# One plain pair instead of two at the start of the feed-forward, and three weight-sum jobs that begin when the sliding stage's caches are loaded

## The reference

```
h = x @ w_in                                  # q/k/v of both attentions, two gates
A = differential attention (8 heads), B = sliding-window attention (16 heads, 2 kv heads)
x = LayerNorm(ALPHA * x + (sigmoid(g_a) * (A @ w_branch_a) + sigmoid(g_b) * (B @ w_branch_b)) @ w_o)
x = LayerNorm(ALPHA * x + relu(x @ w_up) ** 2 @ w_down)       # w_up 1024 x 4096, w_down 4096 x 1024
```

## Time and profile before

| | |
|---|---|
| median of three runs | 2153.51 us (2150.11 to 2153.92) |
| the profiled execution | 2153.98 us, its span 2152.2 us |
| TensorE (PE) busy | 2122.7 us, 99% of the span |
| VectorE (DVE) busy | 1470.2 us, 68% |
| ScalarE (ACT) busy | 1229.0 us, 57% |
| GpSimd (POOL) busy | 65.2 us, 3% |
| DMA | 399.27 MB, mean 186 GB/s |
| mean granted TensorE clock | 0.994 of full speed |

### The profile page before, as it was taken

The page is one execution under the profiler, slowest core; times in us unless marked ns, Lnnn a source line. Parts: engine busy times, 40 slices in busy tenths (PEclk is TensorE's granted clock), DMA queues, the critical chain, the costliest instruction groups (busy, mean ns, idle before and its releaser), DMA issues.

```text
span 2152.2 us, 38215 instructions
## 1 busy us (share of the span) xinstructions
PE 2122.7 (99%) x15004; PEld 1940.8 (90%) x15004; DVE 1470.2 (68%) x2336; ACT 1229.0 (57%) x2493; POOL 65.2 (3%) x100
## 2 busy tenths in 40 slices
PE   9999999999999999999999999998899999999998
PEld 7998889999989898989889888898899898989897
DVE  6757778667879356665767677785668793566646
ACT  4457776587535356656234677674875353556561
POOL 1000000000000000000010000000000000000000
PEclk9999999999999999999999999999999999999999
DMA  8876567984351855454268775479842517554541
GB/s 262 246 271 251 209 240 208 269 261 109 94 186 45 237 155 173 146 170 138 103 215 235 286 253 200 182 230 258 242 119 84 186 57 230 158 171 153 171 148 69
DMA packets 100866, 399.27 MB, mean 186 GB/s; under 512 B 15272, under 2 KB 16936, under 8 KB 87600
## 3 DMA queue, kind: packets, MB, share of 16 engines
q1 hardware_dynamic: 67904, 191.55, 26.0%
q0 software_dynamic: 7936, 92.28, 17.2%
q10 hardware_dynamic: 24848, 112.99, 14.7%
HBM read 367.42 MB, written 118.23 MB: 226 GB/s over the span
## 4 chain that ended last, share of the span: by engine, by line
PE 93%; DMA 2%; ACT 2%; issue 1%; DVE 1%; ACTq 0%; DVEq 0%
PE PS L828 9%; PE PS L830 8%; PE PS L829 8%; PE PS L1049 7%; PE PS L1050 7%; PE PS L1051 7%; PE PS L917 5%; PE PS L918 5%; PE PS L919 5%; PE PS L987 3%; PE PS L988 3%; PE PS L989 3%; PE PS L861 3%; PE PS L863 3%; PE PS L862 3%; PE PS L1177 2%
## 5 line engine op out<-in xcount | busy, mean ns | idle before, releaser
L828 PE MATMUL PS<-xt_hi,w_hi 128*128 128x320 f32 x1184 | 384.2, 325 | 8.8 <-ACT rope_s L1628 8.6
L830 PE MATMUL PS<-xt_hi,w_lo 128*128 128x320 f32 x1184 | 367.6, 310 | 0.0
L829 PE MATMUL PS<-xt_lo,w_hi 128*128 128x320 f32 x1184 | 367.5, 310 | 0.0
L2541 DVE TENSOR_TENSOR w_lo<-w_raw,w_hi 128x1024 fp32r<-128x1024 f32 x146 | 176.7, 1221 | 149.0 <-ACT w_hi L1579 147.6
L2548 DVE TENSOR_TENSOR w_lo<-w_raw,w_hi 128x1024 fp32r<-128x1024 f32 (+1 forms) x176 | 199.2, 1138 | 114.9 <-ACT w_hi L1595 114.6
L1579 ACT ACTIVATE w_hi<-w_raw 128x1024 fp32r<-128x1024 f32 x146 | 152.8, 1059 | 175.5 <-PE PS L1051 155.6
L828 PEld LDWEIGHTS PS<-xt_hi,w_hi 128*128 128x128 f32 x1184 | 224.6, 190 | 14.3 <-ACT rope_s L1628 9.0
L829 PEld LDWEIGHTS PS<-xt_lo,w_hi 128*128 128x128 f32 x1184 | 224.9, 190 | 0.1
L830 PEld LDWEIGHTS PS<-xt_hi,w_lo 128*128 128x128 f32 x1184 | 224.1, 189 | 0.0
L1595 ACT ACTIVATE w_hi<-w_raw 128x1024 fp32r<-128x1024 f32 (+1 forms) x176 | 172.2, 985 | 86.1 <-PE PS L989 66.3
L1049 PE MATMUL PS<-w_hi,act_a_hi 128*128 128x512 f32 x480 | 187.6, 391 | 0.0
(11 more groups left out here) (391 smaller groups left out, 5096.7 us busy)
## 6 DMA issues: line engine op xcount, KB each, us to landing
w_raw<-in_weights SPq DMA_DIRECT2D x186, 512.0 KB, 5.0
kc<-in_k_cache ACTq DMA_DIRECT2D x32, 1024.0 KB, 7.8
vc<-in_v_cache ACTq DMA_DIRECT2D x16, 2048.0 KB, 8.7
w_raw<-up_sums SPq DMA_DIRECT2D x112, 256.0 KB, 2.9
up_sums<-in_up_blocks POOLq DMA_DIRECT2D x24, 1024.0 KB, 10.4
w_raw<-in_up_blocks SPq DMA_DIRECT2D x84, 256.0 KB, 2.8
down_sums<-in_down_blocks POOLq DMA_DIRECT2D x16, 1024.0 KB, 8.8
w_raw<-in_down_blocks SPq DMA_DIRECT2D x32, 512.0 KB, 3.5
```

The source lines that it names most:

```text
L828: mm(out, wh, hi[:, k, c], start=(k == 0), stop=False)
L829: mm(out, wh, lo[:, k, c], start=False, stop=False)
L830: last = mm(out, wl, hi[:, k, c], start=False, stop=(k == KT - 1))
L2541: v.tensor_tensor(w_lo[slot][:], raw[:, raw_of(s, n)[0], :], w_hi[slot][:].bitcast(F32), ALU.subtract)\
```

## The change

`PLAIN_PAIRS` becomes 1: pair 1 of part 0 is computed as a combined pair, so part 0 has one plain and three combined pairs, its up job sums three pairs instead of two, and the second plain pair's two weight tiles leave the stream. ScalarE and VectorE get a new order at the start of the feed-forward. Down 1, and with it up 2 and down 2 behind it, waits for `swa_cache_loaded` in place of `dec_pv`.

```diff
-PLAIN_PAIRS = 2
+PLAIN_PAIRS = 1
...
                 elif (kind, part) == ("down", 1):
-                    pool.wait_ge(dec_pv, 2 * HEADS * (l + 1))
+                    pool.wait_ge(swa_cache_loaded, 32 * (l + 1))
...
                 if i < RING_SLOTS:
-                    act.wait_ge(chunk_done[slot // 3], nth(l, AT_FF) + (1 if slot < 2 else 2))
+                    act.wait_ge(chunk_done[slot // 3], nth(l, AT_FF) + 1)
...
                 g = ring_pair(l, 0, PLAIN_PAIRS)
+                t_high(l, 1, 1)
                 up_tile(l, 0, 0)
-                t_high(l, 1, 1)
-                up_tile(l, 0, 1)
-                ring_high(g)
                 t_high(l, 1, 2)
                 t_high(l, 1, 3)
-                up_tile(l, 1, 0)
+                ring_high(g)
+                up_tile(l, 0, 1)
                 ring_high(g + 1)
-                up_tile(l, 1, 1)
                 ff_seed(l, 0, PLAIN_PAIRS, 0)
                 ring_high(g + 2)
                 t_high(l, 1, 4)
...
                 g = ring_pair(l, 0, PLAIN_PAIRS)
                 x_sums(l, 1, 1)
-                low(0, nth(l, AT_FF, 1))
+                x_sums(l, 1, 2)
+                x_sum_low(l, 1, 1)
                 up_tile_low(0, 0)
-                x_sums(l, 1, 2)
-                low(1, nth(l, AT_FF, 1))
+                x_sums(l, 1, 3)
+                ring_low(g)
                 up_tile_low(0, 1)
-                ring_low(g)
-                x_sum_low(l, 1, 1)
-                x_sums(l, 1, 3)
                 x_sum_low(l, 1, 2)
+                x_sum_low(l, 1, 3)
                 ring_low(g + 1)
-                x_sum_low(l, 1, 3)
-                up_tile_low(1, 0)
                 ring_low(g + 2)
                 x_sum_low(l, 1, 4)
                 ring_low(g + 3)
-                up_tile_low(1, 1)
                 wait_apart(dve, ln_rows, ROW_STEPS * (l + 1))
```

## The result

The changed kernel takes 2162.83 us (median of 7 runs, 2157.99 to 2170.12), the kernel before 2153.92 us in the same rounds (7 runs, 2150.11 to 2157.53): ratio 1.0045, 95% interval 1.0025 to 1.0065. It is slower by some 9 us. The forecast was 2150.5 us; the time lies above its range of 2143 to 2162. The profiled execution took 2162.83 us with a span of 2161.0 us, so the two spans differ by 8.8 us.

The account below looks back on a forecast made before the run. The prediction took TensorE, busy for 2122.7 of 2152.2 us, to bound the kernel. It summed 2153.98 + 22.2 (feed-forward) - 25.3 (jobs) = 2150.9 us, as a median 2150.5, with an 8-in-10 range of 2143 to 2162 us.

Parts of the forecast that it names:

- The jobs: Branch A's end: starting down 1 and later jobs after the caches removes TensorE's waits and slow clock, -25.3 us net.
- rival A: Branch A's end: s_v's issue stays long without the jobs, because of s_k's 256-byte runs; 2163 us, chance 0.13.
- the doubling: Branch A's cache loads: s_k's 256-byte runs could need twice a weight tile's time, 7.4 us, keeping about 2 us wait per layer.
- The moved jobs in branch B: Sliding stage and branch B: the jobs moved there were allowed 1.5 us for both layers.
- Rival C: Branch B: moved jobs make gate loads late as in branch A, 9.5 us more than allowed; 2160 us, chance 0.12.
- The feed-forward: Feed-forward start: fewer matmuls, but TensorE stands 10.9 us before the combined pair; +11.1 us a layer, +22.2 for both.
- The clock after it: Feed-forward, after the new stall: TensorE restarts at half speed for 4.0 us, losing 2.0 us a layer.
- Rival D: Feed-forward: the stall is covered in some unseen way, so the change is all gain there; 2125 us, chance 0.03.
- B: Branch A and feed-forward: all 27.8 us go and the clock costs nothing after the new idle time; 2146 us, chance 0.22.
- Up 0's longer job: Layers' starts: up 0 takes 6 or 7 us more and up 1 ends later, around 120 us; costed at nothing.
- Slower: Whole kernel: a time over 2157.8 us, carried by rival A and half of Rival C, chance 0.19.

Follow-up runs that it names:

- e2: The changed kernel with down 1 back on the old wait, dec_pv (feed-forward change alone): 2182.86 us, ratio 1.0125 to the kernel before.
- e9: The changed kernel with the last pair of part 1 summed by up 2 instead of up 1: 2163.3 us, ratio 1.0039 to the kernel before.
- e6: The kernel before, two plain pairs, with up 1 and the jobs behind it waiting for swa_cache_loaded: 2149.91 us, ratio 0.9977.
- e4: The changed kernel with the feed-forward's preparation reordered, first combined product's needs first on ScalarE and VectorE: 2157.84 us, ratio 1.0015 to the kernel before.
- e5: The changed kernel with up 1 also waiting for swa_cache_loaded, so four jobs run late: 2165.51 us, ratio 1.006 to the kernel before.
- e7: The kernel before with up 1 waiting for dec_pv and down 1 for swa_cache_loaded, two plain pairs: 2133.78 us, ratio 0.9904.
- e8: The changed kernel with e4's order and up 1 waiting for dec_pv, down 1 for swa_cache_loaded: 2152.73 us, ratio 0.9989 to the kernel before.
- e1: The kernel before with only down 1's wait moved to swa_cache_loaded, two plain pairs kept: 2130.28 us, ratio 0.9889.
- e3: e1 with up 0 also summing the first pair of part 1, three pairs in all: 2140.78 us, ratio 0.9932 to the kernel before.

## Why the prediction was wrong, point by point

1. **The jobs, -25.3 us: right.** The stages from branch A to LayerNorm gave 26.4 us (12.3 + 14.1). The four waits of L861 went as the loads' slack said. In the same stage `s_v`'s issue took 1.4 us in place of 4.8 to 8.0. The view of all issues of that line in the changed kernel (duration in ns, least, median, most):

```profile
L2431 ACTq DMA_DIRECT2D s_v<-in_swa_vc x2: 1373/1422/1472, 429.5 to 1504.1; - x2
```

That refutes rival A: the issue is short without the jobs. With the old wait, in e2, it took 1.6 us in layer 0, where the DMA share during it was 0.44, and 5.3 in layer 1, where it was 1.00. `s_k` landed in 5.1 to 5.3 us, against my 4.2. The Trainium skill, page "DMA: Bandwidth & Descriptors", section "Specifications", says that pieces under 512 bytes are read, modified and written. It gives no factor; the doubling, to an estimate of 7.4 us, was mine. Measured were 5.3 us in layer 0, and a weight tile of the same size, issued beside it, took 5.3 us as well (the median of the stage was 3.7). So the short runs cost nothing here beside a load in long runs. That is one pair of loads, and it does not bear the rule out. I had kept 1 us of wait for both layers; there was none.

2. **The moved jobs in branch B: right, with a limit.** I allowed 1.5 us; the wait of L1049 was 1.4 us, and the branch itself had none, with a DMA share of 0.80. Rival C's late load did come: one gate load of branch B took 12.3 us (issued at 561.64). But this gate was wanted so much later that ScalarE stood for 0.2 us and TensorE not at all. What I had not seen is how near the edge the stage behind it is: with one pair or one job more, w_o's weight tiles are late, as e9 and e6 show.

3. **The feed-forward, +22.2 us: right.** Measured 22.6. The chain on VectorE ran as it was laid out, from the second step of `x_sums` on (at 671.76 us). Its last five instructions in layer 0, and TensorE, which stood for 10.72 us (forecast 10.9):

```profile
676.10 1.48 DVE L3133 TENSOR_TENSOR t_lo<-t,t_hi 128x1280 fp32r<-128x1280 f32 x1
677.50 0.82 DVE L3507 TENSOR_TENSOR act_a_lo<-rope_c,act_a_hi 128x640 fp32r<-128x640 f32 x1
678.24 1.48 DVE L3125 TENSOR_TENSOR t<-xt_hi,t 128x1280 f32<-128x1280 f32 x1
679.75 1.49 DVE L3127 TENSOR_TENSOR t<-t,xt_lo 128x1280 f32<-128x1280 f32 x1
681.16 1.22 DVE L2546 TENSOR_TENSOR w_lo<-w_raw,w_hi 128x1024 fp32r<-128x1024 f32 x1
```

```profile
682.43 0.64 PE L929 MATMUL PS<-xt_hi,w_hi 128*128 128x320 f32 x1 [10.72 <-DVE w_lo L2546]
```

The clock after it, in two windows of the changed kernel:

```profile
683.00:687.00 4.00, 4.00 (x17) 4.00 (x16) 4.00 (x4) 0.69 (x2) 0.00 (x0) 0.50 0.41 131
687.00:688.00 1.00, 1.00 (x7) 1.00 (x6) 0.33 (x2) 1.00 (x2) 0.00 (x0) 0.69 0.00 0
```

From the restart at 682.43 the clock stayed at 0.50 until within the microsecond from 687, about 5 us, of which half is lost: some 2.5 us where I had taken 2.0. Rival D falls with it, and of B only the first half came: of the 27.8 us at branch A's end nothing stayed (26.4 net, with 1.4 of new wait at L1049). e4 shows what order can do about the stall: 13.0 us in place of 21.4.

4. **Up 0's longer job: the step that failed.** I wrote: "Up 0 sums three pairs instead of two, 40 us by 6 or 7 more, at the layers' starts, and up 1 ends that much later, around 120 us; TensorE does not wait there now and I cost it at nothing." The consequence was seen and the delay was of the right kind (8.5 us in layer 0, 105.31 to 113.83; in layer 1 18 us, 1174.08 to 1192.05, of which 6 are the layer's own later start). The cost was wrong: 12.0 us in place of nothing. That TensorE does not wait now was no reason. The question was by how much the keys were in time, and that was 0.9 us for the second load of layer 0. The other question was what is issued between the old end of the job and the new one, 115.2 and 126.3 us by the landing of its last transfer: the two key loads, the first that TensorE needs after a change of stage. 6.0 us of wait followed. The lower clock was the rest: in layer 0 5.35 us busy at 0.50 in the windows above is 2.7 us lost, and with the 3.5 us of wait there 6.2, against 6.3 in the table.

It was also the one mechanism with a sign against the change which I had dropped without a rival. With 12.0 added, the sum would have been 2162.9 us as a profiled time and 2162.5 as a median, against the measured 2162.8. Such a close fit is partly luck: the other terms were off by -1.1, +0.4 and +0.6 us, which nearly cancel.

5. **The chances.** "Slower" had 0.19, carried by A and C, and neither happened. The range reached up to 2162 only for their sake; that the time came out less than 1 us above it is not to the reasoning's credit.

**What stays open.** That the transfer's share of the DMA engines, and not some other effect of GpSimd's later end, delays the keys rests on the queue's share beside the landing times (none, in e5, e7 and e8: 6.8 to 7.1 us; 0.4%, e9: 7.0; 12.3%, before: 9.5; 26.9%, e1: 10.1; 36.1 to 37.4%, in e2, e3, the changed kernel and e4: 11.3, 14.2, 14.5 and 16.5), and on e3, e5, e6, e8 and e9. At nearly the same share, 36.1 to 37.4%, the landings lie up to 5 us apart, so the share alone does not tell the landing. It was not tried with a transfer of another kind in its place. Nor was a version tried in which the key loads are issued earlier.

## What to carry to other kernels

When a change lengthens background work, "nobody waits there now" prices nothing: list the transfers issued between its old end and its new one, and read the slack of each, first of all those at a change of stage. Late us on the engine that bounds the kernel can cost more than themselves, since the clock can fall with the stop: 6.0 us of wait cost 12.0 at the keys, 10.7 some 13 at the first combined pair, and e1's 1.7 no more than itself. And the instruction that a wait is named after need not be the late one: in e6 it was `rows`, and the late load stood two engines before it. And where one change holds two effects near 25 us that nearly cancel, measure each half alone: here one half by itself was 1.1% faster, and the other 1.3% slower.

## What the runs showed of the hardware

- **Short stops were enough to lower the clock.** After waits of 1.88 and 1.64 us at 128 to 133 us the granted clock was 0.50 for six us; after a single one of 1.67 us in layer 1 of e1 the mean over its 50 us was still 1.00, and in layer 1 of the changed kernel, after one of 2.5 us, it was 0.93. In e4 stops of 3.62 us at 675 and 681 were followed by a mean of 0.95 over 32 us. The length of the wait alone does not tell the cost.
- **The issue of a load holds ScalarE's queue by the load of the machine:** `s_v`'s two issues took 4.8 and 8.0 us before, with a DMA share of 0.99 during both, and 1.4 and 1.5 us in the changed kernel, at 0.27 and 0.44; in e2 they took 1.6 at 0.44 and 5.3 at 1.00.
- **Loads beside GpSimd's copies and accumulating transfers landed late:** 2.10 MB of GpSimd's queue in 22 us stood beside 1 MB loads of 14.5 us; 0.02 MB beside 7.0 us. Those 2.10 MB held 36.5% of the engines' time, 17% a MB, where the busiest other queue held 40.5% for 3.56 MB, 11% a MB.
